# Loading and squaring the first half's rows in the mixing stage, and sharing the exact copies between ScalarE and VectorE when the feed-forward stage opens

## The reference

```python
mix = concat([rms_scale(y_attn), rms_scale(y_sgu), rms_scale(y_ssm)]) * branch_norm_g
h = h + mix @ w_out                          # the mixing stage writes this
u = rms_norm(h, norm_ffn_g) @ ffn_w_up       # 1024 -> 2 * 2816
u = causal_depthwise_conv(u, ffn_conv_w) + ffn_conv_b
val, gate = split(u)
h = h + (gelu(gate) * val) @ ffn_w_down
```

## Time and profile before

| what | value |
|---|---|
| median of 3 runs | 2857.06 us (2857.01 to 2857.15) |
| profiled execution | 2857.93 us, of which the span is 2856.3 us |
| TensorE, share of the span busy | 91% |
| VectorE, ScalarE, POOL | 60%, 48%, 18% |
| mean granted clock of TensorE | 0.958 |
| last product of the mixing stage starts | 1169.76 us |
| first product of the feed-forward stage starts | 1213.25 us |

### The profile page before, as it was taken

How to read it: one execution, slowest core, us unless ns; L and a number is a source line. 1 busy time by engine, 2 the same in 40 slices (tenths; PEclk the granted TensorE clock), 3 DMA queues, 4 the chain that set the end, 5 groups by cost and what they waited for, 6 DMA issues and landing times. The chain is left out here.

```text
span 2856.3 us, 38966 instructions
## 1 busy us (share of the span) xinstructions
PE 2593.2 (91%) x13883; PEld 2231.7 (78%) x13883; DVE 1710.5 (60%) x3358; ACT 1369.0 (48%) x2460; POOL 509.4 (18%) x309
## 2 busy tenths in 40 slices
PE   6999997999835699579999999999999999997998
PEld 5989986999834588468888878888888878885876
DVE  1110271777686777388888755578888864444333
ACT  3343332666522566355555455455555543334444
POOL 3454453766300121000000000000000000000000
PEclk9999998999968799789999999999999999998999
DMA  4665456888332354312222266642222236753221
GB/s 161 195 220 170 155 166 158 180 184 184 92 104 77 118 173 154 112 52 74 89 89 82 89 225 231 235 162 84 74 89 89 82 137 240 269 195 107 75 73 47
DMA packets 313911, 392.11 MB, mean 137 GB/s; under 512 B 22161, under 2 KB 222161, under 8 KB 310650
## 3 DMA queue, kind: packets, MB, share of 16 engines
q1 hardware_dynamic: 299850, 341.60, 39.1%
q0 software_dynamic: 13888, 48.25, 4.3%
HBM read 298.59 MB, written 95.33 MB: 138 GB/s over the span
## 5 line engine op out<-in xcount | busy, mean ns | idle before, releaser
L2365 PE MATMUL ffn_bank<-ffn_x,ffn_ring 128*128 128x512 f32 x880 | 345.9, 393 | 20.5 <-DVE ffn_ring L2159 14.3
L2366 PE MATMUL ffn_bank<-ffn_x,ffn_ring 128*128 128x512 f32 x880 | 345.1, 392 | 0.0
L2367 PE MATMUL ffn_bank<-ffn_x,ffn_ring 128*128 128x512 f32 x880 | 345.1, 392 | 0.0
L504 ACT ACTIVATE att_exps<-att_scores,att_part 128x256 f32<-128x256 f32 (+1 forms) x384 | 153.1, 454 | 125.4 <-DVE att_part L475 123.7
L2365 PEld LDWEIGHTS ffn_bank<-ffn_x,ffn_ring 128*128 128x128 f32 x880 | 167.0, 190 | 57.3 <-DVE ffn_ring L2159 9.3
L475 DVE CUSTOM_DVE_ANT_0 att_scores<-att_bank,att_bias 128x256 f32<-128x256 f32 (+1 forms) x384 | 122.5, 363 | 142.2 <-PE att_bank L422 67.7
L2432 POOL DMA_DIRECT2D ffn_act<-ffn_late x88 | 47.6, 541 | 859.5 <-DVE ffn_late L2211 859.5
L2198 DVE SCALAR_TENSOR_TENSOR ffn_strips<-ffn_strips,ffn_taps 128x512 f32<-128x512 f32 x176 | 132.0, 750 | 114.4 <-ACT ffn_strips L2009 114.4
L938 POOL TENSOR_TENSOR in_w_lo<-in_w,in_w_hi 128x2048 fp32r<-128x2048 f32 x36 | 166.0, 4612 | 183.3 <-ACT in_w_hi L821 183.3
L2366 PEld LDWEIGHTS ffn_bank<-ffn_x,ffn_ring 128*128 128x128 f32 x880 | 167.1, 190 | 35.0
L2367 PEld LDWEIGHTS ffn_bank<-ffn_x,ffn_ring 128*128 128x128 f32 x880 | 166.8, 189 | 34.9
(11 more groups left out here) (337 smaller groups left out, 6984.0 us busy)
## 6 DMA issues: line engine op xcount, KB each, us to landing
ffn_w<-in_ffn_w_up SPq DMA_DIRECT2D x88, 512.0 KB, 4.8
ffn_a_raw<-ffn_act SPq DMA_DIRECT2D x176, 256.0 KB, 5.9
ffn_w<-in_ffn_w_down SPq DMA_DIRECT2D x40, 1024.0 KB, 6.9
in_w<-in_w_in SPq DMA_DIRECT2D x36, 1024.0 KB, 6.2
ffn_act<-ffn_late POOLq DMA_DIRECT2D x88, 256.0 KB, 2.7
mixed_part<-branch_results SPq DMA_DIRECT2D x16, 792.0 KB, 5.4
z_rows<-in_result SPq DMA_DIRECT2D x80, 128.0 KB, 2.3
branch_results<-att_part SPq DMA_DIRECT2D x8, 1056.0 KB, 9.7
```

What stands on the lines that cost most here:

```text
L504: nc.scalar.activation(exps[:, n % RING, m * width:(m + 1) * width], scores[:, n % RING, m * width:(m + 1) * width], ACT.Exp, bias=part[:, ...
L2365: pe.matmul(out[:, :], hi[:, k], x_hi[kind][:, k], start=(k == 0 and fresh), stop=False, skip_group_check=not fresh)
L2366: pe.matmul(out[:, :], hi[:, k], x_lo[kind][:, k], start=False, stop=False, skip_group_check=not fresh)
L2367: mm = pe.matmul(out[:, :], lo[:, k], x_hi[kind][:, k], start=False, stop=(k == KH - 1), skip_group_check=not fresh)
```

## The change

SP, having issued its last load of the mixing stage, loads the eight row tiles of the first half back from HBM into the memory of the raw `w_out`, and ScalarE squares them there, at the end of its own list of that stage. The buffer and the mean squares outlive the stage. The feed-forward stage begins with two `scale_rows` one after the other, on these rows. Its memory is laid out anew: kinds 1 and 2 get tiles of their own, kinds 3 and the hi parts of 6 and 7 take the shared 32 KB, where the rows are until they have been turned; `a_raw` lies in one place for the first half and in another for the second. In `split_first_group` ScalarE makes only the rounded copies and, behind VectorE's lo parts, the exact copies for kind 5 (`keep_first_group`); VectorE makes those for kind 4. The turns of the second group's first two blocks stand ahead of the taps, and the copy of the taps behind the first two weight operands.

```diff
+class RowsAhead:
+
+
+    def __init__(self, nc, keep, tiles):
+        self.mean_sq = keep.sb("ahead_mean_sq", [P, tiles])
+        self.loaded, self.mean_ready = keep.sems("ahead_loaded", tiles), keep.sem("ahead_mean_ready")
+        self.tiles, self.rows = tiles, None
...
+            sp.wait_ge(w_lo_ready, KC)
+            for t in range(rows_ahead.tiles):
+                sp.wait_ge(stored[t % 2], (t // 2 + 1) * DMA)
+                sp.dma_start(rows_ahead.rows[:, t], h_tiles[t]).then_inc(rows_ahead.loaded[t], DMA)
...
+            def square_ahead(t):
+                act.wait_ge(rows_ahead.loaded[t], DMA)
+                if t:
+                    act.wait_ge(rows_ahead.mean_ready, t)
+                nc.scalar.activation(squares[:, :], rows_ahead.rows[:, t], ACT.Square, scale=D ** -0.5,
+                                     accum_out=rows_ahead.mean_sq[:, t:t + 1]).then_inc(rows_ahead.mean_ready, 1)
...
+                    if last and j >= 2:
+                        for t in range((j - 2) * RING, (j - 1) * RING):
+                            square_ahead(t)
...
+    KEEP_ORDER = (2, 3, 0, 1)
...
-        halves_of = shared.rearrange("p (o s k t) -> p o s k t", o=2, s=2, k=KH)
-        own, exact = {}, {}
-        for kind in (3, 4, 5, 6, 7):
-            own[kind] = st.sb(f"x{kind}", [P, 2, KH, BANK], F32R)
+        x_hi, x_lo, exact = {}, {}, {}
+        for kind in (1, 2, 4, 5):
+            own = st.sb(f"x{kind}", [P, 2, KH, BANK], F32R)
+            x_hi[kind], x_lo[kind] = own[:, 0], own[:, 1]
+            if kind in (4, 5):
+                exact[kind] = st.over(f"exact{kind}", [P, KH, BANK], F32, nc.sbuf_base - KH * BANK * 4)
+        spare_later = st.over("a_raw_later", [P, RAW, BANK], F32, nc.sbuf_base - 2 * KH * BANK * 4)
+        spare = st.over("a_raw", [P, RAW, BANK], F32, shared_at + 2 * KH * BANK * 4)
+        a_raw = [spare, spare_later]
+        quarters = shared.rearrange("p (s k t) -> p s k t", s=4, k=KH)
+        x_hi[3], x_lo[3], x_hi[6], x_hi[7] = (quarters[:, n] for n in range(4))
+        for kind in (6, 7):
+            x_lo[kind] = st.sb(f"x_lo{kind}", [P, KH, BANK], F32R)[:, :, :]
...
-            if h == 0 and grp == 1:
-                return late.rearrange("p t n -> p (t n)")[:, t * D:(t + 1) * D] if t < 2 else plain[:, (t - 2) * D:(t - 1) * D]
+            if h == 0:
+                return rows_ahead.rows[:, grp * TILES + t]
...
-            load_rows(0, 0)
-            load_rows(0, 1)
...
-            def split_first_group(h, k):
-                one, two = turn_banks(h, 0, k)
+            def round_first_group(h, k):
                 act.wait_ge(transposed, h * TG * KH + k + 1)
-                for src, chunk, kind, kept in ((one, k, 1, 5), (two, KH + k, 2, 4)):
-                    nc.scalar.activation(exact[kept][:, k], src[:, :], ACT.Identity, scale=g_cols[:, chunk:chunk + 1])
+                for src, chunk, kind in zip(turn_banks(h, 0, k), (k, KH + k), (1, 2)):
                     nc.scalar.activation(x_hi[kind][:, k], src[:, :], ACT.Identity, scale=g_cols[:, chunk:chunk + 1]).then_inc(hi_written, 1)
+
+            def keep_first_group(h, k):
+                act.wait_ge(lo_written, h * LO_HALF + 2 * k + 2)
+                nc.scalar.activation(exact[5][:, k], turn_banks(h, 0, k)[0][:, :], ACT.Identity, scale=g_cols[:, k:k + 1]).then_inc(x5_kept, 1)
...
-            for t in range(TILES):
-                square(0, 0, t)
             root(0, 0)
+            root(0, 1)
             act.wait_ge(gain_loaded, DMA)
             for k in range(KH):
-                split_first_group(0, k)
-            for t in range(TILES):
-                square(0, 1, t)
-            root(0, 1)
+                round_first_group(0, k)
+            for k in KEEP_ORDER:
+                keep_first_group(0, k)
...
+                                round_first_group(h + 1, TURN_AT.index(f))
+                                keep_first_group(h + 1, TURN_AT.index(f))
...
+                if h:
+                    dve.wait_ge(mean_ready, (grp + 1) * TILES)
+                else:
+                    dve.wait_ge(rows_ahead.mean_ready, (grp + 1) * TILES)
+                squared = mean_sq[:, n] if h else rows_ahead.mean_sq[:, grp * TILES:(grp + 1) * TILES]
+                nc.vector.tensor_scalar(mean_sq[:, n], squared, EPS, None, ALU.add).then_inc(eps_added, 1)
...
+                nc.vector.tensor_scalar(exact[4][:, k], turn_banks(h, 0, k)[1][:, :], g_cols[:, KH + k:KH + k + 1], None, ALU.mult).then_inc(x4_kept, 1)
...
             scale_rows(0, 0)
+            scale_rows(0, 1)
             dve.wait_ge(gain_loaded, DMA)
             for k in range(KH):
                 split_first_group(0, k)
-            dve.wait_ge(taps_turned, 1)
-            nc.vector.tensor_copy(taps[:, :, :], bank[3][:, 0:N_TAPS * 2 * F].rearrange("p (n f) -> p n f", f=2 * F)).then_inc(taps_ready, 1)
-            scale_rows(0, 1)
+            for k in KEEP_ORDER:
+                keep_first_group(0, k)
             sum_weights(0, 0, 0)
             sum_weights(0, 0, 1)
             for j in range(2):
                 split_operand(0, j)
+            dve.wait_ge(taps_turned, 1)
+            nc.vector.tensor_copy(taps[:, :, :], bank[3][:, 0:N_TAPS * 2 * F].rearrange("p (n f) -> p n f", f=2 * F)).then_inc(taps_ready, 1)
...
                 if h == 0 and grp == 1 and k < 2:
-                    pe.wait_ge(lo_written, 2 * (k + 2) + 2)
+                    pe.wait_ge(x5_kept, KEEP_ORDER.index(k + 2) + 1)
+                    pe.wait_ge(x4_kept, KEEP_ORDER.index(k + 2) + 1)
...
                 if h and grp == 0 and k >= 2:
                     pe.wait_ge(lo_written, h * LO_HALF + 2 * (k - 1))
+                    pe.wait_ge(x5_kept, h * KH + k - 1)
+                    pe.wait_ge(x4_kept, h * KH + k - 1)
...
+                if h == 0 and j < 3:
+                    pe.wait_ge(x5_kept, KEEP_ORDER.index(0 if j == 0 else 1) + 1)
+                    pe.wait_ge(x4_kept, KEEP_ORDER.index(0 if j == 0 else 1) + 1)
...
                 turn(0, 0, k)
+            turn(0, 1, 0)
+            turn(0, 1, 1)
             pe.wait_ge(taps_loaded, 2 * DMA)
-            pe.wait_ge(lo_written, 2 * KH)
+            pe.wait_ge(x5_kept, KEEP_ORDER.index(1) + 1)
+            pe.wait_ge(x4_kept, KEEP_ORDER.index(1) + 1)
             for n in range(N_TAPS):
                 mm = pe.transpose(bank[3][:, n * 2 * F:(n + 1) * 2 * F], tap_rows[:, n, :], ident[0:2 * F, 0:2 * F])
             mm.then_inc(taps_turned, 1)
-            turn(0, 1, 0)
-            turn(0, 1, 1)
...
-            w_out = st.sb("w_out", [P, KC, D])
+            w_out = st.sb("w_out", [P, KC, D], align=LINE)
+            shared_at = nc.sbuf_base - KC * D * 4
+            rows_ahead.rows = st.over("rows_ahead", [P, KC, D], F32, shared_at)
```

More of the change, by code:

```diff
@@ L1917, in square @@
                 n = (h * TG + grp) * TILES + t
-                act.wait_ge(rows_loaded[grp][t], rows_count(h, grp))
+                act.wait_ge(rows_loaded[grp][t], DMA)
+                n -= TG * TILES
                 if n >= 2:
@@ L1980, in split_a @@
                     act.wait_ge(conv_ready, (h * F + F - 1) * 4)
-                nc.scalar.copy(a_hi[a % RING], a_raw[:, a % RAW]).then_inc(a_hi_ready, 1)
+                nc.scalar.copy(a_hi[a % RING], a_raw[h][:, a % RAW]).then_inc(a_hi_ready, 1)
             def keep(h, f, kind):
@@ L2712, in hybrid_block @@
         bands_stored = whole.sem("bands_stored")
+        rows_ahead = RowsAhead(nc, whole, KC)
         ssm = {k[4:]: v for k, v in w.items() if k.startswith("ssm_")}
```

36 lines of the change are left out of this document (18 added, 18 removed).

## The result

| | before | after |
|---|---|---|
| median of 6 runs each | 2857.11 us (2855.16 to 2860.3) | 2839.97 us (2838.52 to 2840.6) |
| profiled span | 2856.3 us | 2839.0 us |
| ratio, 95% interval | | 0.9938 (0.9925 to 0.9951) |

The change makes the kernel 17.1 us faster by the medians and 17.3 us by the two spans; 17.4 were forecast, and 2839.7 us.

The account below looks back on a forecast made before the run. VectorE's list was taken to limit the feed-forward opening; its terms put the second group 17.4 us earlier. 2857.93 less 17.4 is 2840.5; with the median 0.87 below the profiled run, 2839.7 us, range 2837.0 to 2844.0.

Parts of the forecast that it names:

- Loads and squares in the mixing stage cost nothing: End of the mixing stage: eight loads and squares done by 1166.5, with 3.7 us of cover before the last addition.
- Start at 1177.4, 0.1 behind SP: Feed-forward opening: VectorE begins at about 1177.4, close to SP's 1177.29; bounds 1177.2 and 1177.9.
- Two scalings 6.8: First in VectorE's opening list: two scalings in a row, 3.39 us each, 6.8 together, until 1184.2.
- Eight lo parts 5.4: Next in VectorE's opening list: eight lo parts, 0.67 us from start to start, 5.4 together, until 1189.6.
- Four copies 2.4, range 1.4 to 2.7: VectorE's opening list: four exact copies, new there, taken at 0.60 us each like an addition reading PSUM; until 1192.0.
- Sums 2.66, operands and taps 1.54: End of VectorE's opening list: four weight sums 2.66 us, two operands 1.2, copy of the taps 0.34.
- The sum: VectorE's opening list added up: its second group begins at 1196.2 instead of 1213.64, 17.4 us earlier.
- The gain's landing: Feed-forward opening: the gain's transfer, needed at 1182.9; landings up to about 1183.4 cost nothing.
- rival (a): Feed-forward opening: the gain lands at 1185.1 and everything is 1.6 us later, 2841.3 us; chance 0.25.
- Rival (b): TensorE's clock stays low through products 0 and 1, 5.1 us each; costs 3.3 us, 2843.0 us; chance 0.10.
- Rival (d): Second half's first group, in the down-projection: ScalarE's copies wait for lo parts and hold TensorE; slower, 2867.7 us; chance 0.02.
- VectorE's list carries the whole rest forward: From VectorE's second group on: whatever brings it forward brings the whole rest of the kernel forward by as much.

Follow-up runs that it names:

- gain_ahead: The changed kernel, but SP loads the gain in the mixing stage behind the eight row tiles, instead of POOL in the feed-forward stage; 2838.81 us, ratio 0.9943.
- changed_again: The changed kernel as it is, run once more on the chip of three of the variants; 2841.33 us, ratio 0.9947 to before.
- gain_by_sp: The changed kernel, but SP instead of POOL loads the gain, first in its list of the feed-forward stage; 2841.70 us, ratio 0.9948.

## Why the prediction was right

- *Loads and squares in the mixing stage cost nothing.* Right. Squares went at 1.25 us each (1153.35 to 1162.07 is seven of them), and the last addition waited 4.68 us for TensorE with them and without. It came 7.11 us before SP's first issue, as before, and in the nine experiments that distance is 7.10 to 7.15.
- *Start at 1177.4, 0.1 behind SP.* It was 0.05.
- *Two scalings 6.8.* 7.2: 3.77 from the first eps to the second (1176.34 to 1180.11), and 3.43 from there to the lo parts. The first was slowed by POOL's issue (0.45), and 0.13 is the wait for the gain; no row of before had a scaling and such an issue side by side.
- *Eight lo parts 5.4.* 5.27. *Four copies 2.4, range 1.4 to 2.7.* 2.64 (1188.81 to 1191.45), 0.66 each: a product with a column of scalars went at the pace of the lo parts (0.66), not at that of the additions (0.60). The row it should have been taken from is the one with the same kind of operand.
- *Sums 2.66, operands and taps 1.54.* 2.65 and 1.45 (1194.10 to 1195.55).
- The sum was 17.4 for the second group; measured 17.09. Scalings (0.4) and copies (0.24) were longer, start, lo parts, operands and taps together 0.3 shorter.
- *The gain's landing.* 5.9 us from the issue; landings up to 6.1 us after SP's start were to cost nothing, and it came at 6.4, so rival (a) came with 0.13 us of its 1.6.
- *Rival (b)* came in part: product 0 took 5.28 us where 5.1 was its price (read from a window whose mean clock was 0.66, so a little low), product 1 was fast again; cost 0.87, not 3.3. The forecast gave it a chance but no share in the sum. The mixing stage's 1.00 us stood against it by luck, so that 2839.7 came closer than its terms did.
- *Rival (d)* put the danger in waits of TensorE. VectorE's waits for ScalarE stayed (10.1 us), and TensorE's for activations are as short as before.
- *VectorE's list carries the whole rest forward.* Right in every run: from the second group to the seventh product it is 27.41 to 27.43 us wherever TensorE doesn't come late, and from there to the end 1612.9 to 1615.4 with no pattern by variant, a scatter of 2.5 us that is larger than some of the effects above.
- *Not said in the prediction:* that the copies' sharing between the engines is worth nothing. It put four copies at 2.4 us into VectorE's list, which sets the time, but never asked for the time with all eight on ScalarE behind the lo parts: 18.44 against 19.26.

## What to carry to other kernels

When a stage opens with loads and statistics of data that an earlier stage has long written, look for the earlier stage's idle ends of SP, ScalarE and VectorE, and for memory that is dead by then; here loads and squares gave 10.8 us and the scaling another 3.5. Then write down the list of the engine that limits the opening and ask of every item whether an idle engine can take it: giving it work to relieve an engine that isn't the limit (the copies) was a small loss, and taking four sums off it gave back 2.58 of their 2.65 us.

## What the runs showed of the hardware

- VectorE's scaling of four tiles of 128x1024 float32 in SBUF took 3.19 us where it began beside a transfer that POOL was issuing (0.92 us), and 2.74 us in every kernel where it didn't: 0.45 us for one issue, all of it in the first instruction (1.21 us instead of 0.75). The Trainium skill's page "Advanced Engine Details and Errata" (VectorE Performance Modes, Mode Summary) says that VectorE's second SBUF port is shared with GpSimd, so that GpSimd's instructions and VectorE's two-port ones get in each other's way. The trace agrees in that VectorE is slowed, with this price; that the port is the reason no row shows.
- The same 4 KB of single numbers landed 2.4 us after SP's issue ahead of the first weights, 5.9 us after POOL's issue behind them, and 14.7 us after SP's issue behind the eight row tiles (gain_ahead).
- Four sums of 128x512 float32 took POOL 1.26 to 1.29 us each, about twice VectorE's 0.66. VectorE's lo parts and copies beside them, which read PSUM, took what they took without (4.04 us for six, 2.72 for four); its two subtractions in SBUF, of which the first overlapped POOL's last sum by 0.2 us, took 0.08 us more.
- Product 0 took 5.28 us where all of it lay at the lower clock (changed, changed_again and gain_by_sp), 4.24 to 4.70 where its first 3.0 to 4.0 us did, and 3.0 where none did. The length of TensorE's wait just before it, 0.18 to 2.74 us, doesn't sort these times.
